# Five weight panels of the modulation moved from the two expert-router stages into earlier gaps of a Trainium2 kernel

## What is computed

```python
# first part, i = 0, 1
m = mixer(rms_norm(x, gains[i, 0]))
x = x + rms_norm(m, gains[i, 1])
f = conv_ffn(rms_norm(x, gains[i, 2]), ...)
x = x + rms_norm(f, gains[i, 3])
# second part, i = 0, 1
mod = silu(c) @ w_ada[i] + b_ada[i]            # 1024 -> 6*1024
sh1, sc1, gt1, sh2, sc2, gt2 = split(mod, 6)   # and the same for the context's c_ctx
h = rmsnorm(x, g1[i]) * (1 + sc1) + sh1
x = x + gt1 * mixed_branches(h)
h2 = rmsnorm(x, g2[i]) * (1 + sc2) + sh2
aff = softmax(h2 @ w_router[i]); gate, idx = top_k(aff.T, 32)
x = x + gt2 * experts(h2[idx], gate)           # w_e1, w_e3, w_e2: 16 x (1024 x 1024) each
```

## Time and profile before

| | before |
|---|---|
| median of 3 runs (lowest, highest) | 2777.91 us (2774.27, 2778.23) |
| the profiled execution | 2774.08 us |
| its span (first to last instruction) | 2772.2 us |
| mean granted TensorE clock | 0.953 of full speed |
| TensorE matmul busy | 2528.3 us, 91% |
| DVE, ACT busy | 978.3 us, 459.0 us |
| read from HBM | 661 MB |

### The profile page before, as it was taken

How to read it: one execution, slowest core, us unless ns; L and a number is a source line. 1 busy time by engine, 2 the same in 40 slices (tenths; PEclk the granted TensorE clock), 3 DMA queues, 4 the chain that set the end, 5 groups by cost and what they waited for, 6 DMA issues and landing times.

```text
span 2772.2 us, 33055 instructions
## 1 busy us (share of the span) xinstructions
PE 2528.3 (91%) x14191; PEld 1721.0 (62%) x14191; DVE 978.3 (35%) x1970; ACT 459.0 (17%) x1008; POOL 60.6 (2%) x91
## 2 busy tenths in 40 slices
PE   8999999999999999999989998887999998676666
PEld 6678887668887877767774333333788885232322
DVE  2535501345513876654451211112574322110101
ACT  1320001131102122232121111113021211000001
POOL 1010000000000100000000000000100000000000
PEclk9999999999999999999999999999999999776776
DMA  8676444484444311112559999999414278999997
GB/s 304 228 188 181 157 152 148 141 273 149 150 157 140 114 61 61 61 61 69 205 213 409 417 422 421 421 421 341 131 60 172 102 291 348 421 421 421 420 421 314
DMA packets 202981, 664.42 MB, mean 240 GB/s; under 512 B 14226, under 2 KB 60596, under 8 KB 153940
## 3 DMA queue, kind: packets, MB, share of 16 engines
q1 hardware_dynamic: 193952, 641.97, 60.5%
q0 software_dynamic: 8688, 20.28, 2.7%
q10 hardware_dynamic: 196, 0.06, 0.0%
HBM read 661.12 MB, written 9.57 MB: 242 GB/s over the span
## 4 chain that ended last, share of the span: by engine, by line
PE 73%; DMA 21%; DVE 3%; ACT 1%; issue 1%; ACTq 0%; DVEq 0%; SPq 0%
PE ps L553 27%; DMA ring<-in_w_e 21%; PE ps L611 16%; PE ps L1298 9%; PE ps L824 5%; PE ps L574 3%; PE ps L1248 2%; PE ps L1275 1%; PE ps L796 1%; PE ps L1091 1%; PE ps L1043 1%; PE ps L1056 1%; PE ps L1113 1%; PE ps L715 1%; PE ps L1031 1%
## 5 line engine op out<-in xcount | busy, mean ns | idle before, releaser
L1298 PE MATMUL ps<-ring,arena 128*32 128x256 f32 (+1 forms) x4344 | 593.8, 532 | 175.0 <-DMA ring<-in_w_e 166.9
L553 PE MATMUL ps<-normed,ring 128*128 128x256 f32 x2624 | 579.8, 382 | 7.2 <-ACT normed L2429 3.5
L553 PEld LDWEIGHTS ps<-normed,ring 128*128 128x128 f32 x2624 | 497.8, 191 | 83.4 <-issue 7.2
L1298 PEld LDWEIGHTS ps<-ring,arena 128*32 128x32 f32 (+1 forms) x4344 | 195.1, 134 | 553.4 <-DMA ring<-in_w_e 261.7
L611 PE MATMUL ps<-ring 128*128 128x256 f32 x912 | 208.7, 383 | 3.3 <-DVE ring L1774 3.3
L553 PE MATMUL ps<-arena,ring 128*128 128x256 f32 (+1 forms) x704 | 198.5, 438 | 1.3 <-DVE small L1426 1.3
L611 PEld LDWEIGHTS ps<-ring 128*128 128x128 f32 x912 | 173.8, 192 | 30.4 <-issue 7.2
L611 PE MATMUL ps<-normed,ring 128*128 128x256 f32 x768 | 171.6, 380 | 0.1
L553 PEld LDWEIGHTS ps<-arena,ring 128*128 128x128 f32 x704 | 131.9, 190 | 57.6 <-issue 42.7
L611 PEld LDWEIGHTS ps<-normed,ring 128*128 128x128 f32 x768 | 144.4, 190 | 21.3 <-issue 1.7
L824 PE MATMUL ps<-arena,ring 128*128 128x256 f32 x704 | 152.3, 379 | 0.0
(11 more groups left out here) (303 smaller groups left out, 2274.7 us busy)
## 6 DMA issues: line engine op xcount, KB each, us to landing
ring<-in_w_e SPq DMA_DIRECT2D x363, 1024.0 KB, 20.3
ring<-in_w_in SPq DMA_DIRECT2D x56, 1024.0 KB, 5.3
ring<-in_w_ada SPq DMA_DIRECT2D x48, 1024.0 KB, 7.4
ring<-in_ffn_w_up SPq DMA_DIRECT2D x88, 512.0 KB, 6.4
ring<-in_ffn_w_down SPq DMA_DIRECT2D x22, 1024.0 KB, 5.0
ring<-in_dil_w_qkv SPq DMA_DIRECT2D x18, 1024.0 KB, 5.1
arena<-in_w_e SPq DMA_DIRECT2D x16, 1024.0 KB, 12.5
ring<-in_sb_w_qkv SPq DMA_DIRECT2D x12, 1024.0 KB, 14.7
```

The costliest lines, as they stand in the source:

```text
L553: ins = mm(o[:, 0:n], slots[k // 4][:, k % 4, f * P:(f + 1) * P], src[:, k, 0:n], start=k == 0, stop=k == kts - 1)
L1298: ins = mm(o[w * g:w * g + w, 0:cols], lhs(2 * c + j), part, start=c == 0 and j == 0, stop=c == KT // 2 - 1 and j == 1)
```

## The change

Five panels leave the router stages (3 in layer 0, 2 in layer 1). The gaps after the mixers get 2 panels each instead of 1, the gaps after the feed-forward networks 2 and 5 instead of 1 and 3. So there are 7 groups instead of 9, still 24 panels and 610 chunks. In the list of chunks the first expert chunks follow `w_out` directly; the load of the last aside chunk of each layer is moved to stand 9 ring places behind `w_out`'s end, and the stretch with 6 slots in layer 0 is drawn over the first six expert chunks, as it covered six chunks of panels before. Since a group can now lie across both layers' panels, `ada_columns` works out layer and column for each panel.

```diff
-ADA_FIRST, ADA_SECOND, ADA_MIXER, ADA_BLOCK, ADA_ROUTER, ADA_LAYER = 3, 6, 1, (1, 3), (3, 2), 4
-ADA_GROUPS = (ADA_FIRST, ADA_MIXER, ADA_BLOCK[0], ADA_SECOND, ADA_MIXER, ADA_BLOCK[1], ADA_ROUTER[0], ADA_LAYER, ADA_ROUTER[1])
+ADA_FIRST, ADA_SECOND, ADA_MIXER, ADA_BLOCK, ADA_LAYER = 3, 6, 2, (2, 5), 4
+ADA_GROUPS = (ADA_FIRST, ADA_MIXER, ADA_BLOCK[0], ADA_SECOND, ADA_MIXER, ADA_BLOCK[1], ADA_LAYER)
...
             panel(a["w_out_2"][i], half * BRANCH)
-        ada_panels(ADA_ROUTER[i])
-        if i == 0:
-            narrow[i] = (narrow[i], len(out))
...
-        early[len(out) + NSLOT - 2 * ADA_ROUTER[i]] = held[then:]
+        early[len(out) + NSLOT] = held[then:]
+        if i == 0:
+            narrow[i] = (narrow[i], len(out) + SUM_SLOT)
...
-        ADA_ROWS = [view(o, 512) for o in [24576, 25088] * 3 + [18944, 0, 19968]]
+        ADA_ROWS = [view(o, 512) for o in [24576, 25088] * 3 + [0]]
...
                 rows = qtiles // 2 * N_EXPERTS
-                ada_parts(ADA_ROUTER[i] - 1)
                 pe.wait_ge(aff_ready.sem, aff_ready.nth("pe"))
...
-                ada_parts()
                 pe.wait_ge(pos_ready.sem, pos_ready.nth("pe"))
...
-                ada_fold()
                 pe.wait_ge(P_ready.sem, P_ready.nth("pe"))
...
-                i, c = divmod(ada["panel"], N_MOD * D // BRANCH)
+                panels = [divmod(ada["panel"] + n, N_MOD * D // BRANCH) for n in range(count)]
...
-                for n in range(count):
-                    at = 4 * (c + n)
+                for n, (i, c) in enumerate(panels):
+                    at = 4 * c
...
                 ve.tensor_scalar(aw, sc, -1.0, None, ALU.add).then_inc(pos_ready.sem, pos_ready.up())
-                ada_add()
...
                 ins.then_inc(P_ready.sem, P_ready.up())
-                ada_columns()
...
                 stamp().then_inc(tok_ready.sem, tok_ready.up())
-                ada_copy()
```

## The result

| | before | after |
|---|---|---|
| median of 15 runs each (lowest, highest) | 2777.55 us (2772.70, 2779.05) | 2781.20 us (2778.97, 2785.24) |
| ratio after / before, 95% interval | | 1.002 [1.0012, 1.0028] |
| profiled execution, its span | 2774.08, 2772.2 us | 2783.31, 2780.8 us |
| TensorE matmul busy | 2528.3 us | 2522.2 us |
| mean granted clock | 0.953 | 0.953 |

The changed kernel is 0.2% slower (5.6 us by the ratio). TensorE has 6 us less to do and the end comes later. (All fences here are copied from the profiles; L numbers are those of the kernel named, and in the changed one L714 multiplies panels, L738 folds, L1244 is `gather`, L1294 the experts, L2408 and L2410 are ACT's input and squares.)

The account below looks back on a forecast made before the run. Chain 73% TensorE, 21% DMA; before the experts the DMA engines lack room, not time. 2.64 + 2.3 - 0.6 + 0.4 = +4.7 us, on the execution behind the median 2777.91: 2782.6 us, +0.17%; range 2774.5 to 2790.

Parts of the forecast that it names:

- Loads and stock: Expert stages: equal expert chunks on chip at their start, DMA engines idle about 25 us more over both stages; gain 0.
- Router stage 0, removed work: Layer 0's router stage: the removed panels, fold, copy and addition stood beside waits; gain 0.
- Router stage 1: Layer 1's router stage: without the fold, gather starts about 0.6 us earlier; gain 0.6 us.
- the clock's term: Router stages: without panels TensorE's clock falls sooner and gather must bring it back; +0.4 us in all.
- Three small gaps: After both mixers and the first network: one more panel delays ACT's last pair 0.88 us each; 2.64 us.
- The gap after network 2: Two more panels: first product 2.1 us late, w_in's landing hidden, plus 0.2 us for a tenth chunk; 2.3 us, bounds 1.5 and 5.
- the tenth chunk: Gap after network 2: five panels are 10 chunks, the ring has 9 slots; fifth panel waits, 0.2 us taken.

Follow-up runs that it names:

- e7: The kernel before, profiled once more with the program unchanged; one run, 2779.71 us.
- e1: The kernel before with the router stages' five panels left out and put nowhere, gaps as before; 2773.96 us against 2774.47, ratio 1.0001.
- e6: The changed kernel, with SP holding back the chunks behind w_in's first pair until that pair has landed; one run, 2780.28 us.
- e11: The changed kernel with four panel chunks given other slots, so the first w_in pair takes slots of the first and second panel; 2780.42 us, ratio 1.0017.
- e4: The kernel before with five panels in the gap after network 2, one in each mixer's gap, router stages 1 and 2; 2785.31 us, ratio 1.0037.
- e3: The kernel before with 2 panels in each mixer's gap, 1 and 3 after the networks, router stages 1 and 2; 2781.53 us, ratio 1.0023.
- e8: The kernel before with two of the four panels at layer 1's start moved to the mixers' gaps; 2770.71 us against 2776.49, ratio 0.998.
- e10: e3 with five chunks of layer 1 given slots, so the second w_in pair takes slots that panels leave; 2776.95 us, ratio 1.0005.
- e9: The kernel before with one panel moved from router stage 0 to the gap after network 2, four there; 2775.01 us against 2774.55, ratio 1.0004.
- e2: The changed kernel with five panels put back in the router stages too, as work done twice; 2783.58 us, ratio 1.0032.

## Why the prediction was right, and where a step was off

The forecast was 2782.6 us, and +4.7 on one execution; the medians give 2781.2 and +3.7, the ratio with its interval +3.3 to +7.8 us. The shifts that are the change's add up to 2.4 + 3.7 - 0.2 + 0.2 = 6.1 us, and without the two stretches that were set aside the whole shift is 8.57 - 1.75 - 1.68 = 5.1. The 1.0 us between these is the -1.2 of layer 0's experts and the +0.2 at the end. In layer 0's experts every other profile, e7 of the unchanged program among them (0.8), also runs 0.4 to 1.3 us shorter than the profile of before, so this belongs to that profile. That the two medians come within 1.4 us of the forecast is partly luck: by its parts the change costs 1.4 us more than the sum had.

- **Loads and stock: right.** Both stages idle their DMA engines longer, by about 15 us in layer 0 and 10 in layer 1, which is the 25 us of the forecast; the chain meets the loads as long after the experts' start as before, to 0.1 us, and e1 shows it with the gaps untouched. One reading was off: 1568.54 us is where the chain enters a load, and TensorE's first wait for one comes 9 us later. Nothing in the sum hangs on it.
- **Router stage 0, removed work: right** (the stage as a whole moves by -0.2 us, in e1 by +0.1). **Router stage 1: right in the step, lost in the next.** Without the fold `gather` does start 0.6 us earlier against the positions' turn ahead of it. But the affinities' turn, now at half clock, takes 0.2 us more, and `gather` itself runs 0.43 us longer, so the experts start with the same shift as the stage. In layer 0 the affinities' turn costs the same 0.2 us and `gather` is 0.41 us shorter. So the clock's term is -0.2 in layer 0 and +0.6 in layer 1, +0.4 in all as forecast, and with the -0.6 the two terms make -0.2, as forecast. This agreement is luck in part: `gather` of layer 1 took 5.15 us in one profile of the unchanged program and 6.63 in the other (e7), and the terms are smaller than that.
- **The clock.** Before, the engine idled for 4.52 us ahead of the positions' turn (L1232), now it idles nearly from 1437 to 1448 us, and `gather` of layer 0 takes no longer (9.82 us against 10.23). The clock stood at 0.50 at `gather`'s start in both kernels and came back within it in both. By the page "TensorE: Matmul & The Clock Gate" of the Trainium skill (section "What's actually happening") the lower rate is the default that activity lifts; the rows agree in that (0.50 through the idle stretch, full clock again before `gather` ended), and most of the loss was taken already by the kernel before.
- **Three small gaps: right.** 0.80, 0.81 and 0.80 us against 0.88, by the very steps named: first input 1.42 us late, pairs at ACT's own pace, last one 0.81 late. ACT's pair took 1.32 us, not 1.34.
- **The gap after network 2: the term that was mis-sized**, 2.3 us forecast, 3.7 measured. The step that was off is the sentence "alone, a panel chunk needs 5.0 to 5.1 us, so 859.7. I take the latter: hidden behind 861.44". The time of issue was right (854.59 forecast; 858.79 less the shift of 4.15 is 854.64). The landing was not: 8.2 us instead of 5.1. The price of a lone chunk was put on the third of three chunks that are issued within 3.4 us, though the sentence itself had the 7.5 us of the pair before. With 8.2 us, and 0.2 from landing to the product's start, the product comes at 863.0, and that is where it came (867.22 less 4.15 is 863.07). This wait is 1.09 of the 1.4 us that were missing. The other 0.3 is the tenth chunk: it was put at 0.2 us, but with its 0.35 of waiting the panels took 9.34 us and not 5.36 + 3.44, so 0.54 more. Why the pair needs 8.2 us is not settled: e6 shows that it is late without a load behind it too, and of two kernels with the same earlier issue one waits no longer (e11) and one does (e4).

The Trainium skill (page "SBUF — State Buffer", section "The DMA setup-cost knee (why "@ 1 MiB" ≠ asymptote)") gives about 2 us plus the bytes at 436 GB/s for one transfer. Taken over the three chunks, 3.15 MB, as if they were one, that is an estimate of 9.2 us from the first issue to the last landing. The traces have 11.7 (after) and 11.8 us (e6), so the measurement is above it. Put on the forecast's own 851.2 us the estimate gives 860.4, ahead of 861.44, so it would not have warned of the wait either.

## What to carry to other kernels

Before work is moved off a "crowded" stretch, look whether the resource there is short of time or of room: idle DMA engines and a waiting queue ahead of the stage say room, and then taking loads away from it brought nothing here (e1). Work that waits for a partner (ACT's copy behind the last panel) must be priced on the partner's order, not on its own engine, and a load that is issued close behind others must not be priced like a lone one: take the nearest such pair or three in the trace, and leave a microsecond of doubt. In a ring with hand-written order, inserting chunks anywhere changes which slot comes round to every later chunk; check for each urgent load whose slot it takes, and when that one is given back. And a group that stands between two busy products costs its full time: of the places tried here, that was the one worth emptying.

## What was not expected

- **The ring's turn.** The same number of chunks moved by a few places gave +6.8 us at the start of layer 1 (e3, e4), 1000 us away from the edit, and -1.4 us in the gap after network 2 (e3, e8), where the pair of `w_in` got slots that had long been free. With five slots set by hand the 6.8 us went (e10). The changed kernel had no such jump. That is luck: the prediction never looked at it.
- **Landing times of 1 MB chunks**, from issue, in the gap after network 2. 5.0 to 5.4 us alone, 5.2 to 5.8 for the tenth panel chunk, 7.5 to 8.7 for the second of a pair (before, e7, e9), 8.2 to 10.2 for the third of three (after, e2, e4, e6, e11). Holding back the loads behind in the changed kernel did not help (e6). A good 1 us of this is scatter that no run explains.
- **Profiles of one program differ by 5.6 us** (2772.2 and 2777.8 us of span), part of it in short stretches of half clock that fall at different places, 1.5 us of it in one `gather`. A part of 1 us that is read from two single profiles is at the edge of what they can tell.
